# A hybrid decoder step on one core: 128-row values for the leading tokens, the recurrent half first in tile 1, a reordered last tile, and a first expert block issued in halves

## What is computed

```python
xp = concat(meta_tokens, x_prompt)                 # 16 + 512 rows
h  = rms_norm(x, g_mix)
gq, gk, gv, gr, ga, sq, sk, sv = split(h @ w_in)   # recurrent and attention inputs
o_gla, state = gla_chunked(gq, gk, gv, log_sigmoid(ga @ w_a_up + b_a) / 16)
o_swa = softmax_with_sinks(sq @ sk.T / 8 + bias) @ sv    # window of 128 keys, 8 heads, 2 kv heads
x = x + concat(rms_norm(o_gla) * silu(gr), rms_norm(o_swa)) @ w_out
h = rms_norm(x, g_ffn)
gates, experts = softmax(top_4(h @ w_router + b_router))  # 32 experts
x = x + sum_k gates[k] * expert[k](h)     # 1024 -> 2*1024, clamped SwiGLU, -> 1024
y = rms_norm(x, g_final)
```

## Time and profile before

| | us |
|---|---|
| median of 3 runs | 1346.62 (1346.15 to 1347.44) |
| profiled execution, its time | 1341.64 |
| span of the profile | 1339.5 |
| PE busy | 1284.7 |
| DVE busy | 917.7 |
| ACT busy | 285.0 |
| POOL busy | 123.3 |

### The profile page before, as it was taken

The page is one execution under the profiler, slowest core; times in us unless marked ns, Lnnn a source line. Parts: engine busy times, 40 slices in busy tenths (PEclk is TensorE's granted clock), DMA queues, the critical chain, the costliest instruction groups (busy, mean ns, idle before and its releaser), DMA issues.

```text
span 1339.5 us, 21354 instructions
## 1 busy us (share of the span) xinstructions
PE 1284.7 (96%) x6323; PEld 520.6 (39%) x6323; DVE 917.7 (69%) x1876; ACT 285.0 (21%) x542; POOL 123.3 (9%) x226
## 2 busy tenths in 40 slices
PE   8999999999999999997999998899999997999996
PEld 6876565553333333331333332233333332333332
DVE  3216256756977787775787776687777774777778
ACT  4331133433111121111121121121121111121114
POOL 2000000000020110100110101010111100110100
PEclk9999999999999999999999999999999999999999
DMA  9505163068999999999999999999999999999996
GB/s 356 130 4 191 32 207 138 32 267 333 414 387 388 421 421 420 421 421 420 419 399 423 415 422 421 419 421 405 420 415 420 415 421 422 420 400 422 409 415 274
DMA packets 91409, 468.95 MB, mean 350 GB/s; under 512 B 11870, under 2 KB 29520, under 8 KB 41074
## 3 DMA queue, kind: packets, MB, share of 16 engines
q1 hardware_dynamic: 75070, 441.56, 81.2%
q0 software_dynamic: 7360, 16.79, 3.2%
q10 hardware_dynamic: 8948, 10.19, 2.2%
HBM read 614.82 MB, written 28.77 MB: 480 GB/s over the span
## 4 chain that ended last, share of the span: by engine, by line
PE 72%; DMA 21%; DVE 3%; SPq 2%; issue 1%; ACT 0%; DVEq 0%; ACTq 0%
PE ps L2148 35%; DMA raw<-in_w_down_dram 19%; PE ps L2254 17%; PE ps L1810 5%; PE ps L1833 5%; PE ps L2049 3%; SPq L610 1%; DMA raw<-slot_outputs 1%; PE ps L2063 1%; DVE v_gate L1744 1%; PE ps L2004 1%; PE ps L2003 1%; PE ps L1995 0%; PE ps L1912 0%; DMA x_sb<-in_x_prompt_dram 0%
## 5 line engine op out<-in xcount | busy, mean ns | idle before, releaser
L2148 PE MATMUL ps<-raw,xT 128*64 128x512 f32 x2816 | 617.4, 593 | 18.4 <-DMA raw<-in_w_up_dram 17.0
L1620 DVE STREAM_TRANSPOSE xT<-x_hold 32x192 f32<-32x192 f32 (+2 forms) x680 | 274.9, 404 | 154.2 <-PE ps L2148 134.1
L2148 PEld LDWEIGHTS ps<-raw,xT 128*64 128x64 f32 x2816 | 200.0, 137 | 425.3 <-issue 391.7
L2254 PE MATMUL ps<-raw,aT 128*64 128x512 f32 x1408 | 317.0, 595 | 16.0 <-DMA raw<-in_w_down_dram 16.0
L1620 DVE STREAM_TRANSPOSE aT<-act_g 32x256 f32<-32x256 f32 x352 | 223.4, 635 | 63.7 <-PE ps L2254 53.8
L2254 PEld LDWEIGHTS ps<-raw,aT 128*64 128x64 f32 x1408 | 97.8, 137 | 228.2 <-issue 175.0
L1010 ACT ACTIVATE act_s<-act_g 128x512 f32<-128x512 f32 x46 | 29.0, 631 | 632.7 <-DVE act_g L1604 632.7
L562 POOL DMA_INDIRECT slot_outputs<-y_rows,out_idx x44 | 45.4, 1032 | 607.2 <-ACT y_rows L1015 606.3
L1398 DVE STREAM_TRANSPOSE bias_up<-up_cols 128x1024 f32<-128x1024 f32 x46 | 57.3, 1245 | 1.6
L1833 PE MATMUL ps<-w_c_cols,hT 128*128 128x512 f32 x128 | 56.8, 596 | 0.0
L554 POOL DMA_INDIRECT x_rows<-expert_inputs,row_idx x47 | 49.5, 1053 | 74.5 <-DMA expert_inputs<-h 24.9
(11 more groups left out here) (399 smaller groups left out, 897.5 us busy)
## 6 DMA issues: line engine op xcount, KB each, us to landing
raw<-in_w_up_dram SPq DMA_DIRECT2D x356, 1024.0 KB
raw<-in_w_down_dram SPq DMA_DIRECT2D x180, 1024.0 KB, 10.4
slot_outputs<-zeros ACTq DMA_DIRECT2D x1, 8320.0 KB, 28.1
ahead<-in_w_up_dram SPq DMA_DIRECT2D x8, 1024.0 KB
raw<-slot_outputs SPq DMA_DIRECT2D x8, 1024.0 KB, 16.0
w_c_cols<-in_w_in_dram SPq DMA_DIRECT2D x1, 4096.0 KB, 30.9
w_out_sb<-in_w_out_dram SPq DMA_DIRECT2D x1, 4096.0 KB, 13.7
w_a_cols<-in_w_in_dram SPq DMA_DIRECT2D x1, 2624.0 KB, 12.8
```

Source lines behind the costliest of these rows:

```text
L1620: dve.transpose(dst_at(rows_out, group), src_at(rows_in, parity)).then_inc(done, 1)
L2148: ins = mm(ps[SUB * i:SUB * i + SUB, banks[bank], :], rows_in[:, j, :], weights[:, c:c + HF], start=False, stop=(j == at_end), skip_group_ ...
L2254: ins = mm(ps[SUB * i:SUB * i + SUB, 2, :], aT[:, j, r, :], raw[:, units[j], D * r + HF * i:D * r + HF * i + HF], start=False, stop=(j == ...
```

## The change

Five edits:

- `weigh` uses all 128 rows of `pT` and `sv` for tile 1 too. What lies beyond the live rows is cleared: `sv` of tile 0 among the constants, `pT` of two quarters on POOL once the projections are done. ScalarE waits for these clearings before it fills either.
- DVE takes the recurrent half of tile 1 and its variance ahead of `residual(0)`.
- Last tile: ScalarE copies the logits' parts ahead of the attention's root; DVE makes the early list before the attention's variance and gives the first indices before the scaling; PE turns the second half of mix four products later (after the find and three of them).
- First block: a unit's products are issued in halves, with h2's turning, the router, the parts' sum, the positions and the find between them; DVE computes `shifted` straight from PSUM, ahead of the full position table.
- Turned rows: from the second block on the half with units 4 to 7 is turned and copied first, and the products of the units 4 to 7 wait for that half alone.

```diff
@@ -420,7 +420,7 @@
...
-        NCONST = 16 + 2 * NTILE
+        NCONST = 17 + 2 * NTILE
         def pair_bank(t):
@@ -461,6 +461,7 @@
...
         THIRD_BANKS = (3, 4)
+        TURN_ORDER = ((0, 1), (1, 0), (1, 0))
@@ -519,6 +520,7 @@
...
             made.do(pool.memset(gates[:], 0.0))
+            made.do(pool.memset(sv[:, 0, :], 0.0))
@@ -530,6 +532,8 @@
...
             made.do(pool.memset(chosen[:, 0], 0.0))
+            made.do(pool.memset(pT[:, 0], 0.0))
+            made.do(pool.memset(pT[:, 2], 0.0))
             pool.drain().then_inc(mixer_left, 1)
@@ -868,6 +872,7 @@
...
                 own.step(act.activation(gate[0:SMALL, 0, half], ps[QUAD[2 + i], 4, 0:256], ACT.Copy))
+            act.wait_ge(consts, NCONST)
             own.step(act.activation(sv[0:SMALL, 0, :], ps[0:SMALL, 5, 0:P], ACT.Copy))
@@ -962,8 +967,8 @@
...
             def take_turned(b, dst):
-                for a in range(2):
-                    act.wait_ge(x0_psum, 2 * b + a + 1)
+                for n, a in enumerate(TURN_ORDER[b]):
+                    act.wait_ge(x0_psum, 2 * b + n + 1)
                     for h in range(2):
@@ -973,6 +978,7 @@
...
                     clear_slots()
+                    act.wait_ge(consts, NCONST + 4)
                     move_pT(1)
@@ -989,9 +995,9 @@
...
                 take_h2T(t)
+                take_parts(t)
                 if t == PT - 1:
                     swa_root(PT)
-                take_parts(t)
                 gate_powers(t)
@@ -1453,10 +1459,13 @@
...
             mask_gla(1)
+            take_gla(1)
+            gla_variance(1)
             for t in range(PT - 1):
                 residual(t)
-                take_gla(t + 1)
-                gla_variance(t + 1)
+                if t:
+                    take_gla(t + 1)
+                    gla_variance(t + 1)
                 take_attention(t + 1)
@@ -1473,13 +1482,13 @@
...
             take_attention(PT)
-            swa_variance()
             take_mixT(PT, (0,))
...
             route_experts(PT - 1)
+            early_list()
+            swa_variance()
+            indices(0)
             make_swa_mix(PT)
-            early_list()
-            indices(0)
             take_mixT(PT, (1,))
@@ -1528,12 +1537,15 @@
...
             dve.wait_ge(pos_psum, 2)
-            do(dve.scalar_tensor_tensor(pos_table[:], ps[:, POS_BANK, 0:NTILE * NE].rearrange("p (t e) -> p t e", t=NTILE), 1.0,
-                                        m_keep[:], ALU.add, ALU.mult))
-            do(dve.scalar_tensor_tensor(pos_table[:, PT, 0:1], m_keep[:, PT, 0:1], early_pad[:], pos_table[:, PT, 0:1],
-                                        ALU.mult, ALU.add))
-            do(dve.tensor_scalar(shifted[:].unsqueeze(2), pos_table[:, :, 0:1], float(SUB), None, ALU.subtract))
+            told_pos = ps[:, POS_BANK, 0:NTILE * NE].rearrange("p (t e) -> p t e", t=NTILE)
+            do(dve.scalar_tensor_tensor(shifted[:].unsqueeze(2), told_pos[:, :, 0:1], 1.0 - SUB, m_keep[:, :, 0:1], ALU.add,
+                                        ALU.mult))
+            do(dve.scalar_tensor_tensor(shifted[:, PT:NTILE], m_keep[:, PT, 0:1], early_pad[:], shifted[:, PT:NTILE], ALU.mult,
+                                        ALU.add))
             compare(shifted[:].unsqueeze(2))
+            do(dve.scalar_tensor_tensor(pos_table[:], told_pos, 1.0, m_keep[:], ALU.add, ALU.mult))
+            step(dve.scalar_tensor_tensor(pos_table[:, PT, 0:1], m_keep[:, PT, 0:1], early_pad[:], pos_table[:, PT, 0:1],
+                                          ALU.mult, ALU.add))
@@ -1997,10 +2009,9 @@
...
                     pe.wait_ge(pT_copied, 4 * (t - 1) + 2 * g + 2)
-                    n = META if t == 1 else P
                     for i in range(4):
                         dst = ps[:, g, P * i:P * i + P]
-                        mm(dst, pT[0:n, 2 * g, i, :], sv[0:n, t - 1, :], start=True, stop=False)
+                        mm(dst, pT[:, 2 * g, i, :], sv[:, t - 1, :], start=True, stop=False)
                         ins = mm(dst, pT[:, 2 * g + 1, i, :], sv[:, t, :], start=False, stop=True)
@@ -2071,11 +2082,11 @@
...
                 out(1, 1)
-                turn_mix(PT, 1)
+                out(2, 0)
                 find(0, EARLY_TILES)
-                out(2, 0)
                 out(2, 1)
                 out(3, 0)
+                turn_mix(PT, 1)
                 out(3, 1)
@@ -2135,7 +2146,7 @@
...
                 pe.wait_ge(gathered, 16 * b + 16)
-                for a in range(2):
+                for a in TURN_ORDER[b]:
                     for c in range(4):
@@ -2149,13 +2160,24 @@
...
+            def first_half(j, half):
+
+                if j == 0 and half == 0:
+                    pe.wait_ge(up_seeded, 1)
+                if j in (0, 4) and half == 0:
+                    pe.wait_ge(xT_ready, 8 + 2 * j)
+                if half == 0:
+                    pe.wait_ge(landed[j], 32)
+                for i in range(2):
+                    c = FF * half + HF * i
+                    ins = mm(ps[SUB * i:SUB * i + SUB, FIRST_BANKS[half], :], xT_first[:, j, :], raw[:, SLOT[j], c:c + HF],
+                             start=False, stop=(j == UPU - 1), skip_group_check=True)
+                if half == 1:
+                    ins.then_inc(up_used, 1)
+
             def first_up(j):
-                if j == 0:
-                    pe.wait_ge(up_seeded, 1)
-                if j in (0, 4):
-                    pe.wait_ge(xT_ready, 8 + 2 * j)
-                pe.wait_ge(landed[j], 32)
-                up_products(j, xT_first, FIRST_BANKS)
+                first_half(j, 0)
+                first_half(j, 1)
@@ -2169,13 +2191,16 @@
...
             last_mix_out()
-            for j in range(3):
-                first_up(j)
+            first_up(0)
+            first_up(1)
+            first_half(2, 0)
             turn_h2(PT)
-            first_up(3)
+            first_half(2, 1)
             router(PT)
+            first_half(3, 0)
             sum_parts(PT)
-            first_up(4)
+            first_half(3, 1)
+            first_half(4, 0)
@@ -2194,8 +2219,10 @@
...
             ins.then_inc(pos_psum, 1)
-            first_up(5)
+            first_half(4, 1)
+            first_half(5, 0)
             find(1)
+            first_half(5, 1)
             mark_written((0, 1))
@@ -2217,8 +2244,10 @@
...
                 pe.wait_ge(up_seeded, 2)
-                pe.wait_ge(xT_ready, 32)
+                pe.wait_ge(xT_ready, 24)
                 for n, j in enumerate(BY_LANDING):
+                    if n == UPU - AHEAD:
+                        pe.wait_ge(xT_ready, 32)
                     if n in (1, 3):
@@ -2230,9 +2259,10 @@
...
                 pe.wait_ge(up_seeded, 3)
-                pe.wait_ge(xT_ready, 48)
+                pe.wait_ge(xT_ready, 40)
                 for j in units:
                     if j == 0:
+                        pe.wait_ge(xT_ready, 48)
                         pe.wait_ge(ahead_landed, AHEAD_LANDED + 2 * 16 * AHEAD)
```

More of the change, by code:

```diff
@@ L505, in _ @@
             made.do(pool.memset(m_keep[:], 0.0))
-            assert made.n == NCONST - 2 * NTILE - 7
+            assert made.n == NCONST - 2 * NTILE - 8
             for t in range(NTILE):
```

## The result

The change is faster, just inside the fast end of the stated range (1339.8) and below the forecast's own (1340.6 to 1342.8). In the first comparison, on one chip in turn, the kernel before had a median of 1346.15 us (1344.94 to 1347.44, 5 executions) and the changed kernel 1339.83 (1337.34 to 1340.2, 5 executions): ratio 0.995, 95% interval 0.9935 to 0.9965, so 6.3 us less (interval 4.7 to 8.8) where 5.0 was forecast. In a later one it was 1339.59 (8 executions) against 1344.47 (19): 0.9954 [0.9937, 0.9971], or 3.9 to 8.5 us; the two medians alone differ by 4.9. So the time alone doesn't exclude the forecast's 5.0. The profiled execution took 1339.95 us with a span of 1337.8, which is 1.7 less than the 1339.5 of the profile before.

What follows compares the result with a forecast made beforehand. A fixed-rate weight stream bounds the kernel, so only savings before its start or between first and second block count. Terms -4.7, +0.5, -0.8 give -5.0 us: 1341.6 us from a median of 1346.62; range 1339.8 to 1344.5.

Steps and rivals of the forecast that it cites:

- Leading tokens' values with 128 rows: Tile 1's attention value products, all with 128 rows, take 3.57 us instead of 7.32, ending at 192.8 instead of 196.5.
- rival that height doesn't matter: Tile 1's value products stay as they are, the reorder only fills a wait: 1346.3 us in total; chance 5%.
- Recurrent half first in tile 1: DVE takes it before residual(0): h2 0.7 us later, tile 1's projection at 198.35 instead of 203.09, 4.7 us sooner.
- the 13.90: Time in us from tile 1's first value product (189.19) to its projection (203.09) in the profile the forecast used.
- term of 4.7: Tile 1's projection starts 4.7 us sooner, and all of it reaches the start of the weight stream.
- I carry the difference over: Whole kernel: profiled execution forecast at 1336.6 us; the old median's 5 us above its profiled execution is added, giving 1341.6.
- Last tile: POOL's later clearing starts the first block's gather 1.25 us later, so turn_rows(0) and out_psum come 1.1 us later.
- First block in halves: Finer interleaving makes up about 1.1 us for routing; gather(1), needing the stored h, still comes 0.5 us later (0 to 1.1).
- turned order: Second block: PE starts two ScalarE copies earlier, gaining 0.8 us; third block: nothing.
- The clock did not fall again in tile 1: Rival 1: clock granted 0.50 in tile 1 from 192.8 to 198.3, about 2.7 us lost, total 1344.3 us; chance 15%.
- Rival 3: Last tile costs nothing, gather on time or landing sooner, PE's gains there count: -6.2 us, total 1340.4; chance 12%.

Runs made afterwards that it cites:

- woven work: Half of the second full tile's value products woven among state outer products near 100 us: on the changed kernel 1338.38 us, on the kernel before 1345.96 us.

## Why the prediction was right in direction and short in size

**Leading tokens' values with 128 rows** (forecast 7.32 to 3.57 us): right. 3.81 us in the changed kernel, 3.67 with this part alone. The rival that height doesn't matter fell. At full clock a product took 0.42 us in alternation and 0.22 with equal rows, so the 7.32 us would have been some 6.66 (16 times 0.416) at full clock: 3.1 are the alternation's price and 0.7 the clock's. (The prediction has six of the eight pairs started when the clock fell; it was seven.) Two rules were weighed in the prediction. The Trainium skill's "TensorEngine Tiling (Array Packing)" (Key Properties) says that a change of tiling mode drains TensorE. The runs fit that, with a price of 0.2 us per product here; they show the price and not the drain. The Trainium skill's "TensorE: Matmul & The Clock Gate" (LDWEIGHTS) says that a weight load of 32 rows takes as long as one of 128. The trace before agrees: at full clock two loads took 0.29 us with 16 rows and 0.30 with 128. But the time of these products hung on something else. Only the whole was measured: a run of 16-row products that follow each other was not made, so the height by itself is not told from the alternation; the equal loads are all that speaks against the height.

**Recurrent half first in tile 1** (forecast: h2 0.7 later, projection at 198.35, 9.16 us behind the first product): the mechanism is right. h2 began its last pass at 194.55 and was ready at 195.82, 3.76 behind the first product where it was 2.81 (0.95 later); the normalisation began at 4.11 (forecast 4.01), and from there to the projection it took 5.15 us, the forecast's very number. Neither half of the edit does it alone: the order gave nothing, the rows left a wait of 2.42 us and 12.06 in all, both gave 9.25 or 9.26 us in ten of ten profiles that had them. **What failed in size is the other side, the 13.90.** Five profiles with the old tile 1 show 13.90, 15.24, 15.42, 15.44 and 16.64 us, and the forecast was made from the shortest. That profile has 6.8 us of half clock in tile 1, where the others show about 10 or more. From a typical execution the same reasoning gives 15.4 - 9.2 = 6.2 instead of 4.7. The part alone measured 1346.17 - 1340.42 = 5.8 us, interval 4.4 to 8.8: the term of 4.7 was sized too small, and the 4.7 itself is still inside the interval.

**Sum: "I carry the difference over"** is the step of the prediction that failed. The 5.0 us between the profiled execution and the median were treated as a constant that both kernels have. They go with a higher clock in this one execution, and part of the falls that it was spared lies in the very stretch that the change makes shorter. So the spans of the two profiles differ by only 1.7 us, and the medians by 6.3. The forecast had 1336.6 for the profiled execution and 5.0 on top; measured were 1339.95, as this execution had lost some 3 us near 110 us, and a median 0.1 below it. Two errors, 3.3 us one way and 5.1 the other, left 1.8: that the total came so near is in part luck. The table by clock shows the step: the changed kernel's profiled execution (1339.95) lies at its median, the old one's 4.1 below the median of 99. What part of the falls' time belongs to which fall isn't settled: tile 1's 6.2 and the second block's 0.9 would make 7.1 of a typical execution, more than the 5.9 of the pooled medians. The three profiles with woven work have no early fall, but weaving alone made neither kernel's median lower beyond its interval; two of the thirteen profiles without it have none either.

**Last tile** (forecast: out_psum 1.1 later through gather(0), 1.25 late): the wait is there as described, POOL's clearing 2.9 us later relative to the first weight load and gather(0) 1.2 later, at 13.74. turn_rows(0) moved by 0.7 instead of 1.1. But its price is nothing that shows: with the clearing early again the whole chain up to the store of h came 1.4 earlier and gather(1) did not. The 1.1 lies beside the store's wait behind queued weights, which the forecast had for this store (it took gather(1) 0.5 later) and should have carried to its end: the landing went by the bytes ahead and not by the issue. 1 MB less ahead of it brought gather(1) 1.6 earlier (39.12 to 37.51).

**First block in halves** and **turned order.** Forecast + 0.5 and - 0.8, measured 0 and - 0.9: gather(1) at 38.71 and 38.55 against 38.58, and the second block at 47.18 and 47.16 against 48.05, as ScalarE's copies hold it up for 0.58 us instead of 1.38. The forecast said that the halves gain nothing beyond the last tile's loss; their undoing put the index behind by 1.0 and h by 0.5, so index and stored h are nearly level here, and a gain in one alone is hidden by the other. By time, these edits without tile 1's measured 2.2 us (interval 3.5 less to 0.4 more), and 0.9 lies inside that.

**The rivals.** The clock did not fall again in tile 1 (full from 195 to 205 in all ten profiles with both parts). But the forecast's reason, that the thin products ahead of the fall are gone, doesn't carry this: with the 128 rows alone they are gone too and the clock fell, behind the wait for DVE. Rival 3's time of 1340.4 was nearest, and it was right on the last tile's cost, though not on why: the gather did not land at the same time, what hung on it did. Its gain of 0.7 in the last tile isn't there, so its time was near by luck. Another thing was seen that I don't explain: the clock fell in the last tile in four of eight profiles that have DVE's old order there (49.5 to 49.9, or 48.3, to the second block instead of 47.4 to 48.1) and in none of eight with the new one. Eight profiles of each kind are few, no median shows a gain from it, and why it falls in some executions alone is left open.

## What to carry to other kernels

One profile is one draw: before a sum is made against it, compare its mean granted clock with those of the timed executions, and where it is higher, take the stretches that the clock can touch as longer than they are shown. Where small products alternate between two row counts, try padding the short one, but see first what the next engine is busy with when they end: here the padding alone gave 2.0 us (0.4 to 3.9) and 5.8 together with an order that had the next engine free. And where a store lies behind queued weights, see whether it lands by its issue or by those bytes: here time won ahead of it counted only when the queue ahead of it got shorter.

## What the runs showed of the hardware

- A product of 128 columns (two records) took 0.42 us when 16 and 128 rows alternate and 0.22 us when both have 128, at the full granted clock; at half clock it was 0.72 for the alternation. So the alternation made a product 1.9 times as long at full clock, about what half the clock did to the scores (2.00 to between 3.65 and 3.78 us).
- At full clock two weight loads of 128 columns took 0.29 us with 16 rows and 0.30 with 128.
- The granted clock fell from full (2.4 GHz) to 0.50 (1.2 GHz) during the alternating products of tile 1 in five of five profiles that had them, without them but behind a wait of 2.42 us in the one that had 128 rows alone, and in none of ten with both parts of the edit. It fell near 110 us, during the state outer products, in eleven of sixteen profiles, in some executions of a kernel and not in others.
- Over 99 executions of one kernel, 0.001 of mean granted clock went with 1.2 us of 1346: (1348.19 - 1342.56) over the distance between the two groups' mean clocks, 0.9906 and 0.9953.
- A store of h issued 1.4 us earlier landed 0.5 later; issued at that same time with 1 MB less queued ahead it landed 1.7 earlier than that (SP's wait for it ended at 37.5, 38.0 and 36.3 us behind the first weight load).
